# New sequences for the three busy engines inside the mixers of a two-block transformer kernel

## The reference

```python
for l in range(DEPTH):                                   # first block
    y = swiglu(modulate(x, ...), ffn_w13[l, 0], ffn_w2[l, 0]); x = layer_norm(...)
    y = token_mixer(modulate(x, ...), w_in[l], w_out[l], ...);  x = layer_norm(...)
    y = swiglu(modulate(x, ...), ffn_w13[l, 1], ffn_w2[l, 1]); x = layer_norm(...)
for l in range(DEPTH):                                   # second block
    h = hybrid_layer(h, mem, cos, sin, l, ...)
```

```python
o_inter = einsum('bhtk,bhkv->bhtv', qt * exp(bt), state)
attn = einsum('bhtk,bhtsk->bhts', qt, exp(bt_t - bt_s) * kt)     # masked to s <= t
state = exp(b_last) * state + einsum('bhsk,bhsv->bhkv', kt * exp(b_last - bt), vt)
```

## Time and profile before

| | |
|---|---|
| runs | 2108.25, 2099.62, 2087.59 us (median 2099.62) |
| profiled execution | 2101.3 us from its first to its last instruction; no other time of it is known |
| TensorE busy | 2002.5 us of it (95%) |
| VectorE, ScalarE, GpSimd busy | 1575.3, 1073.1, 308.4 us |
| first mixers (two) | 207 us each |
| second mixers (two) | 228 and 226 us |
| chain that ended last | TensorE 76%, VectorE 14%, ScalarE 4% |

### The profile page before, as it was taken

How to read it: one execution, slowest core, us unless ns; L and a number is a source line. 1 busy time by engine, 2 the same in 40 slices (tenths; PEclk the granted TensorE clock), 3 DMA queues, 4 the chain that set the end, 5 groups by cost and what they waited for, 6 DMA issues and landing times.

```text
span 2101.3 us, 39270 instructions
## 1 busy us (share of the span) xinstructions
PE 2002.5 (95%) x16744; PEld 1854.1 (88%) x16744; DVE 1575.3 (75%) x2135; ACT 1073.1 (51%) x1516; POOL 308.4 (15%) x247
## 2 busy tenths in 40 slices
PE   7999989999999999899999999898999997989998
PEld 7999879979998998789889989887899887979996
DVE  6688788766987677688675649886788489758874
ACT  4543365455434443564554435565665375646652
POOL 0200032111000200203011004610120036002100
PEclk9999999999999999999999999899999999999999
DMA  9888743335985677443245663233465533324552
GB/s 378 325 315 330 279 161 132 106 120 203 354 340 205 243 284 303 148 163 122 82 173 207 252 226 118 101 141 115 147 202 193 205 125 141 122 101 161 202 199 80
DMA packets 60381, 409.85 MB, mean 195 GB/s; under 512 B 6896, under 2 KB 6896, under 8 KB 13872
## 3 DMA queue, kind: packets, MB, share of 16 engines
q1 hardware_dynamic: 54000, 384.85, 49.4%
q0 software_dynamic: 5920, 22.07, 3.1%
q10 hardware_dynamic: 288, 0.42, 0.1%
HBM read 404.17 MB, written 3.15 MB: 194 GB/s over the span
## 4 chain that ended last, share of the span: by engine, by line
PE 76%; DVE 14%; ACT 4%; POOL 2%; issue 2%; DMA 2%; SPq 0%; DVEq 0%; POOLq 0%; ACTq 0%
PE ps L713 13%; PE ps L714 13%; PE ps L715 13%; PE ps L757 7%; PE ps L759 6%; PE ps L758 6%; DVE l L601 4%; PE ps L742 2%; PE ps L1725 2%; PE ps L744 2%; PE ps L743 2%; DMA w<-in_stream 2%; PE ps L625 1%; DVE tmp L975 1%; ACT h L586 1%
## 5 line engine op out<-in xcount | busy, mean ns | idle before, releaser
L601 DVE TENSOR_TENSOR l<-w,h 128x2048 fp32r<-128x2048 f32 (+1 forms) x295 | 672.7, 2283 | 150.1 <-ACT h L586 149.7
L713 PE MATMUL ps<-xh,h 128*128 128x256 f32 x2544 | 722.3, 284 | 19.3 <-DVE gq L2423 9.4
L586 ACT CAST h<-w 128x2048 fp32r<-128x2048 f32 (+1 forms) x295 | 557.0, 1893 | 331.4 <-PE ps L759 162.1
L714 PE MATMUL ps<-xl,h 128*128 128x256 f32 x2544 | 713.6, 281 | 0.0
L715 PE MATMUL ps<-xh,l 128*128 128x256 f32 x2544 | 712.9, 280 | 0.0
L713 PEld LDWEIGHTS ps<-xh,h 128*128 128x128 f32 x2544 | 480.4, 189 | 27.6 <-DVE l L601 12.3
L714 PEld LDWEIGHTS ps<-xl,h 128*128 128x128 f32 x2544 | 480.3, 189 | 2.4 <-issue 2.4
L715 PEld LDWEIGHTS ps<-xh,l 128*128 128x128 f32 x2544 | 480.1, 189 | 0.0
L757 PE MATMUL ps<-h,hh 128*128 128x512 f32 x528 | 207.4, 393 | 0.0
L759 PE MATMUL ps<-h,hl 128*128 128x512 f32 x528 | 205.6, 389 | 0.0
L758 PE MATMUL ps<-l,hh 128*128 128x512 f32 x528 | 205.5, 389 | 0.0
(11 more groups left out here) (425 smaller groups left out, 3007.1 us busy)
## 6 DMA issues: line engine op xcount, KB each, us to landing
w<-in_stream SPq DMA_DIRECT2D x361, 1024.0 KB, 4.9
GB<-in_vec POOLq DMA_DIRECT2D x20, 512.0 KB, 5.8
w<-in_stream SPq DMA_DIRECT2D x8, 512.0 KB, 4.1
gate<-in_vec POOLq DMA_DIRECT2D x6, 512.0 KB, 4.0
memf<-in_memT SPq DMA_DIRECT2D x2, 512.0 KB, 6.1
xf<-in_xT POOLq DMA_DIRECT2D x1, 1024.0 KB, 9.5
kv<-mk POOLq DMA_DIRECT2D x2, 512.0 KB, 6.1
kv<-mv POOLq DMA_DIRECT2D x2, 512.0 KB, 8.6
```

The lines of the kernel that those rows point to most:

```text
L586: e.copy(k.H[m % NH][:, 0:z], k.W[n % NW][:, 0:z]).then_inc(k.hi_done, 1)
L601: e.tensor_tensor(k.L[m % NH][:, 0:z], k.W[n % NW][:, 0:z], k.H[m % NH][:, 0:z], SUB).then_inc(k.lo_done, 1)
L713: p.matmul(P[:, 0:T], H[:, r, o], xh[:, r, :], start=r == 0, stop=False)
L714: p.matmul(P[:, 0:T], H[:, r, o], xl[:, r, :], start=False, stop=False)
```

## The change

The six strings are replaced, nothing else. Each holds the same letters as before, as often, in another order; the two layers of a mixer share them. Of the table (24 lines of difference) one line of each sign stands for all:

```diff
@@ -1511,12 +1511,12 @@
 ORDER1 = dict(
-    pe=("rrrrrr tr t t t t t tgr tg tg t t tgggg t tg tb tbgg tggggg tbg tbg tgbbgg tbgggggg t tgbbggm tm tgggggggmgg tg tmg tmg tgm "
...
+    pe=("rrr trr t t t t t trrgrg t tgg t t tgg tg tg tgb tg tggbg tggbb tbg tggggb tbggggbgg t tgbgmg tgm tgggmggggm t tgg t "
...
@@ -2509,12 +2509,12 @@
 ORDER2 = dict(
-    pe=("hhh th td t t t t t t t t t thh t th thhh t thhhhh thhhhh thd thh thhhh t thhddd t thh td th t tdhhdh thdh tdh thdh td td t "
...
+    pe=("t t th td th thh th t th t td thhhh th t thh t thh th th thhh thh t t thdhhhhd thdh t tdh th tdhdh thdh tdh thd thd "
...
```

More of the change, by code:

```diff
@@ L1513 @@
 ORDER1 = dict(
-    pe=("rrrrrr tr t t t t t tgr tg tg t t tgggg t tg tb tbgg tggggg tbg tbg tgbbgg tbgggggg t tgbbggm tm tgggggggmgg tg tmg tmg tgm "
[L1515 to L1519, removed]
+    pe=("rrr trr t t t t t trrgrg t tgg t t tgg tg tg tgb tg tggbg tggbb tbg tggggb tbggggbgg t tgbgmg tgm tgggmggggm t tgg t "
+         "tggmg tgm tgg tgggmgmbommmomm"),
+    dve=("wr wr t t twr trr t trrr wt twgggg twg twg t twtwg tg tbgg t tgg wtggbbggbg tbg wgg tgggg wg wtb tb wgggm tg tmgggg "
+         "wmgg tg twtg tgmgg tgmgg tg tg wmg twgbbgbmgmmm wmm wm"),
+    act=("wwtr wtr trr t twrr t twrr wt tggg wtg tg wtg tg tg t twgggbg tg tgbb wwg t tggbbgbgggggb twgg tb wg tgbgg tg wgg "
+         "tmgmgmmgggm tm wggg twtggmm tg twggggmg t tbg wmm wmm"),
 )
@@ L2511 @@
 ORDER2 = dict(
-    pe=("hhh th td t t t t t t t t t thh t th thhh t thhhhh thhhhh thd thh thhhh t thhddd t thh td th t tdhhdh thdh tdh thdh td td t "
[L2513 to L2517, removed]
+    pe=("t t th td th thh th t th t td thhhhh th t thh t thh th th thhh thh t t thhdhhhhd thdh t tdh th tdhdh thdh tdh thd thd "
+         "td tdhd tdehdhoeoeoeoee"),
+    dve=("t t twwwt t th wthh twh wthhh wthh th wh wh thhhhh wh thhhhhd wtwd t t td th t thh wthd th thdhh th wdhh t t t th tddh "
+         "twh td whhd twthdd whdh wdd te tddh we we twe wee"),
+    act=("twt twt twwthh t t twthh whh wth th th t th th wh th whh thh thdhh wthd thh twh whdh td thh twdhh twhhh twdd th thd th "
+         "wdhh tdd wthh td wd thddd t thedh wwe we weee"),
 )
```

## The result

The changed kernel takes 2116.96 us (median of 9 runs, 2112.39 to 2122.15), the kernel before, with six further runs beside it, 2100.85 (9 runs, 2087.59 to 2109.85). The ratio is **1.0081, 95% interval 1.0058 to 1.0104**: 17 us slower. The profiled execution takes 2118.6 us from its first instruction to its last, against 2101.3.

What follows compares the result with a forecast made beforehand. TensorE, busy 95% of the span, was taken to bound the kernel. Mixer 2's +6.4 and +9.3 and mixer 1's +4.6 gave +20.3: 2121.6 us against the profiled execution, 2120 against the median, range 2092 to 2140.

Steps and rivals of the forecast that it cites:

- The first meeting: Mixer 2, behind tile 11: TensorE waits for the queries' Silu on ScalarE, 8.6 us in layer 0, 9.95 in layer 1.
- the lower bound of 4.6: Mixer 2: least wait of TensorE behind tile 11, set by GpSimd's sum of the keys, ready near 1321.9.
- Tiles 19, 20, 22: Mixer 2, layer 0: new TensorE waits of 1.1 for a bank, 4.9 and 3.1 for lower halves.
- Idle time of the second mixers as a whole: Mixer 2: new waits less old ones, +8.3 and +7.0 by layer, each with −1.85 at the end.
- Clock: Mixer 2: both layers pay 7.5 us for low clock, so 0 in layer 0 and +4.1 in layer 1.
- The end of mixer 2: Scan results copied ahead of a tile's copy on ScalarE shorten the transposes' waits: −1.85 us in each layer.
- Mixer 1: First mixers: small new waits, 1.0 at tile 10 and 0.8 at tile 11 among them; +2.3 a layer, +4.6 us.
- The opening: Start of mixer 1: claimed as long as before to 0.1 us.
- the waits that only change places: Rival, mixer 2: later waits at tiles 20 and 22, 8.0 us a layer, go; 2104 us, chance 0.18.
- the faster case: Rival, mixer 2: Silu ready near 1321, wait behind tile 11 at most 3.9; 2092 us or 2082, chance 0.14.
- More waits in the dense part: Rival, mixer 1's delta rule: misplaced chunks cost 5 to 10 us more a layer; 2130 to 2140, chance 0.14.
- The table switch: Rival, ScalarE: two loads ahead of the Silu each hold it another 1.28 us; 2125 us, chance 0.05.

Runs made afterwards that it cites:

- the Silu first: The change, with one cast and one level exponential with its table load moved behind the queries' Silu on ScalarE: 1.0029 of the kernel before.
- new mixer 1 alone: The kernel before with the change's ORDER1, so mixer 1 has the new sequences and mixer 2 the old ones: 1.0009 of the kernel before.
- the experiment on that part alone: The kernel before with the change's order behind tile 31 of mixer 2 on all three engines: 0.9993 of the kernel before.
- the meeting behind tile 14: The change, with TensorE's first meeting moved back behind tile 14, ScalarE and VectorE as in the change: 1.0018 of the kernel before.
- the old ScalarE order: The kernel before with only TensorE's first meeting moved behind tile 11, ScalarE and VectorE as before: 1.0011 of the kernel before.
- the early exponentials: The change, with ScalarE's next cast ahead of tile 14's copy and the next level's exponentials ahead of tile 14's and 15's copies: 1.0006 of the kernel before.
- both remedies: The change with the old mixer 1, and on ScalarE the queries' Silu and the level exponentials both moved earlier: 0.9968 of the kernel before.

## Why the prediction held, and where it didn't

Forecast 2120, measured 2117; forecast +20.3 for the profiled execution, measured +17.3. The chain of the waits stands, and so do the terms of TensorE's idle time; those of the clock and of mixer 1 came out less well, and their errors cancel in part. That the result is within 1%, at 0.8%, is partly luck: the forecast stood 0.6 us inside that line, and the measured interval reaches across it.

- *The first meeting*: 8.6 forecast, 8.52 measured; layer 1 9.95 and 8.75. Right, and by the chain given (its pieces add up to 6.4 and 2.6 behind 1316.96, not 6.1 and 3.0; the total is the same): with the Silu first the wait falls to the keys' sum's 4.57, the lower bound of 4.6. The profile names no releaser, where `qs` had been expected; the Silu's end 0.1 before it decides.
- *Tiles 19, 20, 22*: 1.1, 4.9, 3.1 forecast; 1.33, 4.30, 2.99 measured. New waits in that stretch of layer 0 17.1 against 18.0.
- *Idle time of the second mixers as a whole*: forecast 8.3 − 1.85 = +6.4 and 7.0 − 1.85 = +5.2; measured +7.3 and +3.7.
- *Clock*: forecast 0 and +4.1; measured −1.6 and +5.0. Right in kind, by other stretches than forecast. From the trace, TensorE's busy time at 0.50 goes from 23.2 to 17.8 in layer 0 and from 14.6 to 26.2 in layer 1; half of the difference is an estimate of what the clock gave or cost, −2.7 and +5.8. In layer 0 the clock fell while TensorE still waited for the first meeting, which cost no work, and the stretch at the last transposes went from 10.2 to 6.8. The profiled execution before had more of the low clock in layer 0 than its order needs: with new mixer 1 alone, whose mixer 2 is the old one, it is 17.8 too. So −1.6 is no effect of the new order that can be relied on.
- *The end of mixer 2*: forecast −1.85. The waits for `do`, 2.3 and 2.3, are 0.4 and 0.4, but others at L1739 took part of it; by the experiment on that part alone, the main wait fell by 1.4. Too large by 0.4, and by 0.7 in layer 0, where a wait for `htmp` grew by 0.3.
- *Mixer 1*: forecast +2.3 each, measured +2.4 and +1.0 in the traces. **This term had no right to its precision.** The opening, put at "as long as before to 0.1", is not constant: with the old sequences and no edit in it, the first mixers were 187.0 to 190.8 us long in the traces of the kernels above, 187.9 in the mean of eighteen; with the new ones they were 188.0 to 190.2, 189.2 in the mean of ten. So about +1.3 a layer, no more than the lengths scatter within either set, and 2.6 where 4.6 was forecast; that layer 0's 2.4 met the forecast is luck. The new waits are there (tile 10 0.42 and 1.11, tile 11 0.55 and none), mostly smaller than the 1.0 and 0.8 forecast, and a wait of tile 8 of 1.23 that was not looked at is gone.
- *The rivals*: the waits that only change places have fallen (the meeting behind tile 14 gives its time back, and the later waits stay); the faster case has fallen, since the Silu starts at 1327.71, not near 1321; even with the old ScalarE order the first meeting waits 5.6, above the 3.9 that was to decide. More waits in the dense part have fallen: mixer 1 grew by 2.4 and 1.0, not by 5 to 10 more. The table switch: the loads at 1323.79, 1326.42 and 1328.79 take 1.28 each, and the first two are followed by their activations 1.29 behind their start, as in the earlier trace rows. The Trainium skill ("ScalarE: Activation LUTs", "What ACT_TABLE_LOAD costs") puts a switch at 2.66 with its drain; the copy ahead of the first load ends at 1323.77, 0.02 before it, so no drain shows on that side either.

## What to carry to other kernels

When an order is changed by hand, follow the slowest short chain first: which activation does TensorE's next step need, and what stands ahead of it in that engine's strict order, table loads and bank copies included. Count the low clock behind a wait with the wait. Behind the waits of tiles 19, 20 and 22, 8.6 us in layer 0, TensorE was busy at 0.50 for 9.2 us, which cost an estimated 4.6 more (half of it); behind the same three in layer 1 of the kernel with the first meeting behind tile 14 it was 3.3, some 1.6 more. So that part varies from one execution to the next. And ask of an instruction that is sometimes twice as long as its twin what the neighbour engine did at its start, before moving anything.

## What the runs showed of the hardware

In these rows a VectorE instruction with its operands in SBUF that begins while GpSimd works ends late, as if it had stood still until GpSimd's was done. In the change, layer 0's first mixer opens with GpSimd 0.24 ahead of VectorE's L615:

```profile
276.46 2.90 DVE L615 TENSOR_SCALAR acc<-w,sc 128x1024 f32<-128x1024 f32 x1
279.40 3.25 DVE L618 SCALAR_TENSOR_TENSOR acc<-w,sc,acc 128x1024 f32<-128x1024 f32 x1
```

```profile
276.22 2.59 POOL L1041 TENSOR_TENSOR x<-R,GB 128x1024 f32<-128x1024 f32 x1 [2.65 <-issue]
278.95 2.61 POOL L1044 TENSOR_TENSOR x<-x,GB 128x1024 f32<-128x1024 f32 x1
```

L615 begins at 276.46 and ends at 279.36, 0.55 behind GpSimd's end (278.81). L618 then meets GpSimd's next one and ends 1.09 behind its end (281.56). In the kernel with the first meeting behind tile 14, whose mixer 1 has the same sequences, L615 and L618 are done in 0.75 and 1.29, GpSimd comes into the middle of L618, and it is GpSimd that takes longer (3.04, against 2.35 to 2.4 for later ones there):

```profile
273.02 0.75 DVE L615 TENSOR_SCALAR acc<-w,sc 128x1024 f32<-128x1024 f32 x1
273.80 1.29 DVE L618 SCALAR_TENSOR_TENSOR acc<-w,sc,acc 128x1024 f32<-128x1024 f32 x1
```

```profile
274.30 3.04 POOL L1041 TENSOR_TENSOR x<-R,GB 128x1024 f32<-128x1024 f32 x1 [4.17 <-issue]
```

Of the four microseconds two come back in TensorE's wait at tile 3, 5.44 in the one and 3.33 in the other; who was first decides it. By the Trainium skill ("SBUF — State Buffer", section "Who interferes with whom") a port pair that VectorE shares with GpSimd is an exclusive lock, held for a whole instruction by whoever issues first. It names a VectorE instruction in a two-port performance mode, and one with two SBUF inputs against a GpSimd instruction that reads SBUF. L618 is of the second kind; that L615, with one tensor and a scalar, is of the first, no run shows. The rows agree with the lock: each VectorE instruction that waits ends its own length (0.75 and 1.29), less 0.2, behind GpSimd's end. By the lengths of the same forms where GpSimd is idle, an estimate of what GpSimd takes of VectorE's time in layer 0's second mixer is 23 to 24 us before the change, and 22 to 23 after.

A kernel's parts that aren't touched vary too: outside the mixers the profiled executions differ by up to 12 us with the same code (span less the four mixers: 1320.2 in the one with the early exponentials, the shortest of its 12 executions, and 1332.4 in the one with both remedies, the longest of its 12), so terms of 1 us are read from the stretch, not from the total.
